# Decay, keys and token tiles moved ahead of the attention stage, recurrence spread along it: one step of a hybrid streaming encoder

## What is computed

```python
hp = ffn_step(hp, ...)                                  # macaron SwiGLU, 1024 -> 2816 -> 1024, layer norm
(q, k, v, qi, ki, wi), rec, gates = mixer_inputs(hp, w_in, lb)   # one projection, 5448 columns
oa   = attend_prompt(q, qi, wi, k, v, ki)               # index scores, top 256 keys per query, softmax over them
orec = recur_prompt(*rec)                               # HGRN2, 4 heads of 128x128 state
hp   = mixer_output(hp, oa, orec, gates, ...)           # rms norm of orec, gates, two projections, layer norm
hp   = ffn_step(hp, ...)

logf = log(lb + (1 - lb) * sigmoid(f));  kk = (1 - lb) * sigmoid(-f);  rq = silu(bq)
b = cumsum(logf)                                        # "decay", restarted in each block of 80 tokens
o = (q k^T * exp(b_t - b_s), causal) v + (q exp(b)) S
S = S * exp(b_end) + (k exp(b_end - b))^T v
```

## Time and profile before

| | us |
|---|---|
| median of three runs (2941.70 to 2948.98) | 2941.75 |
| the profiled execution's own time | 2947.6 |
| its span, first to last instruction | 2945.9 |
| first FFN | 0 to 837 |
| projection, index scores, search | 837 to 1448 |
| mixers | 1452 to 1862 |
| output projections, second FFN | 1862 to 2946 |

### The profile page before, as it was taken

The page is one execution under the profiler, slowest core; times in us unless marked ns, Lnnn a source line. Parts: engine busy times, 40 slices in busy tenths (PEclk is TensorE's granted clock), DMA queues, the critical chain, the costliest instruction groups (busy, mean ns, idle before and its releaser), DMA issues. The chain is left out here.

```text
span 2945.9 us, 41396 instructions
## 1 busy us (share of the span) xinstructions
PE 2730.8 (93%) x16384; PEld 2628.7 (89%) x16384; DVE 1341.0 (46%) x2842; ACT 668.3 (23%) x1135; POOL 485.8 (16%) x175
## 2 busy tenths in 40 slices
PE   8999999999977999999779986799999999999996
PEld 7999999999967799999768974699799999999995
DVE  2333333333254689992165437455543333333335
ACT  3111111111143522221255533200421111111102
POOL 1122111111010011222100002111111111222212
PEclk9999999999988999999859987799999999999998
DMA  4111111111021011232200000522011111111101
GB/s 146 44 43 43 48 55 54 43 43 30 1 71 44 15 44 44 96 95 89 97 1 31 1 1 8 183 75 80 29 44 43 43 43 43 43 43 44 55 16 60
DMA packets 143708, 149.13 MB, mean 51 GB/s; under 512 B 19648, under 2 KB 130336, under 8 KB 143472
## 3 DMA queue, kind: packets, MB, share of 16 engines
q1 hardware_dynamic: 140144, 134.45, 14.8%
q10 hardware_dynamic: 3456, 13.17, 1.1%
HBM read 123.82 MB, written 23.79 MB: 50 GB/s over the span
## 5 line engine op out<-in xcount | busy, mean ns | idle before, releaser
L475 DVE TENSOR_TENSOR ffn_prod<-ffn_gate,ffn_psu 128x384 f32<-128x384 f32 x132 | 69.5, 527 | 799.9 <-ACT ffn_gate L385 793.6
L67 PE MATMUL ffn_psd<-ffn_hid_hi,ffn_dn_hi 128*128 128x384 f32 (+1 forms) x1056 | 353.9, 335 | 12.7 <-DVE y L500 10.9
L67 PE MATMUL ixp_ps<-h_hi,ixp_hi 128*128 128x384 f32 (+1 forms) x1032 | 339.9, 329 | 20.2 <-ACT y L877 11.5
L67 PE MATMUL ffn_psg<-h_hi,ffn_up_hi 128*128 128x384 f32 (+1 forms) x1056 | 346.4, 328 | 8.4 <-DVE ffn_up_lo L400 6.6
L500 DVE TENSOR_TENSOR y<-y,ffn_psd 128x384 f32<-128x384 f32 (+1 forms) x480 | 250.9, 526 | 217.2 <-PE ffn_psd L69 217.2
L385 ACT ACTIVATE ffn_gate<-ffn_psg 128x384 f32<-128x384 f32 x132 | 61.9, 469 | 1259.3 <-PE ffn_psu L69 1259.2
L67 PE MATMUL ffn_psu<-h_hi,ffn_up_hi 128*128 128x384 f32 (+1 forms) x1056 | 344.0, 326 | 0.0
L68 PE MATMUL ffn_psg<-h_lo,ffn_up_hi 128*128 128x384 f32 (+1 forms) x1056 | 343.9, 326 | 0.0
L69 PE MATMUL ffn_psd<-ffn_hid_hi,ffn_dn_lo 128*128 128x384 f32 (+1 forms) x1056 | 343.8, 326 | 0.0
L68 PE MATMUL ffn_psd<-ffn_hid_lo,ffn_dn_hi 128*128 128x384 f32 (+1 forms) x1056 | 343.7, 325 | 0.0
L69 PE MATMUL ffn_psg<-h_hi,ffn_up_lo 128*128 128x384 f32 (+1 forms) x1056 | 343.1, 325 | 0.0
(11 more groups left out here) (299 smaller groups left out, 4995.5 us busy)
## 6 DMA issues: line engine op xcount, KB each, us to landing
ffn_dn_raw<-in_ffn_wd SPq DMA_DIRECT2D x22, 1024.0 KB, 4.9
ffn_up_raw<-in_ffn_wg SPq DMA_DIRECT2D x20, 1024.0 KB, 5.4
ffn_up_raw<-in_ffn_wu SPq DMA_DIRECT2D x20, 1024.0 KB, 7.8
ixp_raw<-in_w_in SPq DMA_DIRECT2D x39, 512.0 KB, 3.8
spill<-y ACTq DMA_DIRECT2D x24, 536.0 KB, 2.7
mo_sig<-spill SPq DMA_DIRECT2D x32, 192.0 KB, 3.8
y<-spill SPq DMA_DIRECT2D x2, 2144.0 KB, 8.3
y<-y_spill SPq DMA_DIRECT2D x1, 4288.0 KB, 15.0
```

Source lines behind the costliest of these rows:

```text
L67: pe.matmul(out, w_hi, x_hi, start=first, stop=False)
L475: dve.tensor_tensor(self.prod[:, k % 2, 0:w], self.gate[:, k % 2, 0:w], self.ps_up[k % banks][:, 0:w], ALU.mult).then_inc(self.prod_done, 1)
```

## The change

- **Projection order**: `PROJECTED` puts f and rq first, then ak, av, aq, ga and three gb, bi, the other gb, bg. The queries are spilled instead of bi; bi stays in SBUF (`c.y[:, 4:8]`), where the recurrence reads it. Still 24 tiles are spilled; the last nine go through a ring of two tiles in what was the search's scratch, and so wait for its end (`searched`).
- **Decay** becomes a class whose sigmoids and logs run on ACT after tile 10 of the projection (`decay`), whose sums run on DVE right after the search, and whose 32 exponentials and scalings are put among the chunks of the last eight tiles (`tail_order`, which PE, ACT and DVE follow). There too are the high and low keys (K) and the 18 key and value transposes (t, six groups, copied by DVE); SP stores the token rows at the end of that stage.
- **Mixers** begin with the first eight parts of the recurrence, then the three cache transposes (c), then attention. SP loads the queries back in three parts. The other 62 recurrence parts are spread evenly up to 94% of the attention's list, and the norm from there to 99%. In the norm ACT squares (q) and DVE multiplies with the gate (g); POOL has no part in it. The mask is no longer stored per head.

```diff
+SP = {"aq": 0, "ga": 4, "gb": 12, "bg": 20}
+PROJECTED = ([("iq", j) for j in range(4)] + [("ik", 0)] + [("f", j) for j in range(4)] + [("rq", j) for j in range(4)]
+             + [("ak", 0), ("av", 0)] + [("aq", j) for j in range(4)] + [("ga", j) for j in range(8)]
+             + [("gb", j) for j in range(3)] + [("bi", j) for j in range(4)] + [("gb", j) for j in range(3, 8)]
+             + [("bg", j) for j in range(4)])
+STEP_TILES = 8
+def tail_order():
+    chunks = [("P", n) for n in range(3 * STEP_TILES)]
+    out = []
+    for q in range(2 * Decay.NQ):
+        out.append(("e", q))
+        if q % 8 == 7:
+            out += chunks[0:3]
+            del chunks[0:3]
+    out += [("G", 0), ("K", 0)] + chunks[0:2]
+    del chunks[0:2]
+    for g in range(6):
+        out += [("t", g), chunks.pop(0)]
+    return out + chunks
+class Decay:
...
+    def grow_quarter(self, act, n):
+        h, t0 = self.quarters[n % self.NQ]
+        act.wait_ge(self.scanned, h + 1)
+        if n >= 2:
+            act.wait_ge(self.scaled, n - 1)
+        act.activation(self.grow[:, n % 2, :], self.fx[:, h, t0:t0 + T // 4], ACT.Exp,
+                       scale=1.0 if n < self.NQ else -1.0).then_inc(self.grown, 1)
...
     @block.scalar
-        for n in range(NI + EARLY // 3, NTL):
+        for n in range(NI + EARLY // 3, FIRST_STEP):
             for i in range(3):
                 drain(n, i)
+            if n == NI + 5:
+                dc.decay(act, s_mm, len(units))
+        for what, n in order:
+            if what == "P":
+                drain(FIRST_STEP + n // 3, n % 3)
+            elif what == "e":
+                dc.grow_quarter(act, n)
...
     @block.vector
+        dve.memset(bit_f[:], 0.0).then_inc(searched, 1)
+        for h in range(BH):
+            dc.sums(dve, h)
+        for what, n in order:
+            if what == "e":
+                dc.scale_quarter(dve, n)
...
-PACE = 1.22
+REC_SHARE, NORM_SHARE = 0.94, 0.99
 def pass_order(att_blocks, n_rec):
-    rec = [("g", h) for h in range(BH)] + [("e", q) for q in range(2 * 4 * BH)] + [("G", 0)]
-    rec += [("k", 0), ("v", 0), ("u", 0)]
+    rec = [("k", 0), ("v", 0), ("u", 0)]
     for m in range(n_rec):
         rec += [("k", m + 1), ("a", m), ("v", m + 1), ("o", m), ("u", m + 1)] if m + 1 < n_rec else [("a", m), ("o", m)]
-    rec += [("n", h) for h in range(BH)]
+    ahead = 8
+    norm = [x for h in range(BH) for x in [("q", h), ("n", h)] + [("r", 3 * h + i) for i in range(3)] + [("g", h)]]
+    out, done, normed = [("Q", 0)] + rec[0:ahead] + [("c", 0)], ahead, 0
     for i, part in enumerate(att):
         out.append(part)
+        while done < len(rec) and done - ahead < (len(rec) - ahead) * (i + 1) / (REC_SHARE * len(att)):
+            out.append(rec[done])
+            done += 1
+        while done == len(rec) and normed < len(norm) * min(1, (i / len(att) - REC_SHARE) / (NORM_SHARE - REC_SHARE)):
+            out.append(norm[normed])
+            normed += 1
+    return out
...
+                r.load_state(sp)
+                for part, spans in enumerate((((Q1, Q1 + QB),), ((Q1 + QB, LP),), ((LP, T), (0, Q1)))):
+                    for a, z in spans:
+                        sp.dma_start(c.aq[:, :, a:z], c.spill[SP["aq"]:SP["aq"] + 4, :, a:z].rearrange("n p t -> p n t")).then_inc(aq_in[part], 16)
```

More of the change, by code:

```diff
@@ L952, in index_and_project @@
     qs_set, dist_set, d = sem("qs"), sem("dist"), sem("d")
-    spilled = [sem(f"spilled{i}") for i in range(3)]
+    spilled, late_spilled = [sem(f"spilled{i}") for i in range(3)], [sem(f"late_spilled{i}") for i in range(2)]
+    searched = sem("searched")
     h_out = [sem(f"h_out{i}") for i in range(3)]
@@ L1000, in _ @@
         for n in range(4, NTL):
+            if n == NI + 6:
+                pool.wait_ge(s_mm, len(units))
+                dc.constants(pool)
             pr.split_lo(pool, n)
@@ L1187, in settled @@
             dve.wait_ge(d, done[0])
+        dc.bounds(dve)
         dve.wait_ge(dist_set, 1)
@@ L1342, in mixers @@
     units = [(b, h) for b in range(len(blocks)) for h in range(HEADS)]
-    NRT = NRB + 1
-    order = pass_order(len(blocks), NRT)
+    order = pass_order(len(blocks), Recurrence.NRT)
     piece_at, turn_at = {}, {}
@@ L1415, in mixers @@
[L1415 to L1423, removed]
@@ L1430, in by_head @@
[L1430 to L1431 removed]
+        Q1 = N_META + QB
         with nc.Block() as block:
@@ L1615, in make_stack @@
                     q0, m = blocks[b][0:2]
+                    for part in range(3 if b >= NB - 1 else 2 if b else 1):
+                        act.wait_ge(aq_in[part], 32 if part == 2 else 16)
                     if b >= 2:
@@ L1666, in _ @@
                 for what, n in order:
-                    if what == "Q" and n >= 1:
+                    if what == "k":
+                        r.keep_keys(act, n)
+                    elif what == "v":
+                        r.keep_values(act, n)
+                    elif what == "q":
+                        for i, (t0, w) in enumerate(CHUNKS):
+                            if n == 0:
+                                act.wait_ge(r.out_done, r.NRT)
+                            else:
+                                act.wait_ge(r_mm, 3 * n + i - 2)
+                            act.activation(sq[:, i, 0:w], rq[:, n, t0:t0 + w], ACT.Square).then_inc(sq_done, 1)
+                    elif what == "Q":
                         make_stack(n)
@@ L1810, in _ @@
                 for what, n in order:
-                    if what == "Q" and n >= 1:
+                    if what == "c":
+                        for m, (src, dst, rows) in enumerate(prep):
+                            dve.wait_ge(kv_mm, m + 1)
+                            dve.tensor_copy(dst, ps_t[m % 2][0:rows, 0:P]).then_inc(kv_done, 1)
+                        dve.tensor_copy(ks_t[:, PAST:NS], c.ak[:, LP:T]).then_inc(kv_done, 1)
+                    elif what == "a":
+                        r.mask(dve, n)
+                    elif what == "u":
+                        r.add(dve, n)
+                    elif what == "o":
+                        r.keep_out(dve, n)
+                    elif what == "Q":
                         stack_rests(n)
```

641 lines of the change are left out of this document (361 added, 280 removed).

## The result

The change takes 2960.13 us (median of 20 runs, 2942.66 to 2966.58) against 2948.55 for the kernel before (20 runs, 2941.20 to 2952.43): a ratio of 1.0041, interval 1.0030 to 1.0051. It is slower by 0.4%, just beyond what can be told from no change, where 2894 and faster were forecast. The profiled execution took 2959.26, its span was 2957.6.

What follows compares the result with a forecast made beforehand. PE bounds the projection's tail, DVE the mixers' start, where PE idles. Mixers ending at 1814 instead of 1862.5 save 48 us: 2947.6 becomes 2899, less 5.9 for the median, 2894; range 2876 to 2909 (0.62).

Steps and rivals of the forecast that it cites:

- does the clock rise early?: Start of the mixers: PE's clock expected up within some 10 us of the first recurrence parts, 1.00 from about 1485.
- one allowance of 7 us for all falls of the clock: Mixers' blocks: some 7 us added for clock falls, moving the recurrence's end from 1751 to 1758.
- The lengths given for the blocks at full clock: Attention blocks in the mixers: lengths without recurrence plus 5.6 us each while it runs, 273.2 us summed to the recurrence's end.
- Tile 10's stall: Projection: PE stalls 0 to 4 us, taken as 3, while drains wait behind the decay work on ACT.
- The tail's stall: Projection's last tiles: PE waits for a drain behind decay sums and exponentials, 0 to 6 us, taken as 2.
- The norm: Mixers' end, on DVE: reciprocals 28.6, scaling 7.1, gates 5, plus waits, 56 us; mixers end at 1814 instead of 1862.5.
- The recurrence's end: In the mixers: last recurrence output at 1758, allowance for clock falls included, against 1792.9 before.
- the forecast's last step: Whole kernel: from 2899 for a profiled execution to 2894, as the earlier one stood 5.9 us above the runs' median.
- The clock stays at 0.50: Rival, mixers' blocks: half speed for three blocks, 2946, no change (0.06); longer, 2970, slower (0.08).
- Coupling: Rival, mixers' units: one part order on three engines makes waits, 15 to 30 us given back, 2909 to 2924; chance 0.24.
- Stalls in the projection: Rival: both projection stalls in full with clock falls behind, 14 us instead of 7, 2901; no separate chance given.
- The change doesn't do what it says: Rival, mixers: a lagging recurrence would keep the norm from beginning at 94%; nothing showed that, no size or chance given.

Runs made afterwards that it cites:

- exp. 10: Combined run of four edits, plus the sample keys' high part and rests moved behind the fourth and fifth query stack: 2896.06 us, 0.9812 of the kernel before.
- exp. 1: Changed kernel with PE's value products of the unit before moved between second and third batch of turned tiles in nine-tile units: 2917.96 us, ratio 0.9897.
- exp. 3: Changed kernel with 18 unneeded identity transposes added in the gap of nine-tile units: 2933.63 us, 0.9947 of the kernel before.
- exp. 2: Changed kernel with the previous unit's value products made once more in the gap of nine-tile units: 2933.94 us, 0.9954 of the kernel before.
- experiment 4: Kernel before, with value products moved ahead of the third batch of turned tiles in nine-tile units: 2929.44 us, ratio 0.9940.
- experiment 6: Changed kernel with the recurrence spread over 70% of the attention's list instead of 94%, the norm over the rest: 2928.91 us, 0.9938 of the kernel before.
- experiment 8: Changed kernel with value products in the gap, tail drains first, recurrence over 70%, decay's sigmoids and logs singly behind drains of tiles 13 to 16: 2891.71 us, 0.9818.
- experiment 5: Changed kernel with the first tile's three drains ahead of the first eight decay exponentials in the last eight projection tiles: 2955.2 us, ratio 1.0026.
- experiment 9: Changed kernel with value products in the gap, tail drains first and decay pieces behind single drains, recurrence still over 94%: 2903.76 us, 0.9843.
- 11: Combined run of four edits, with the recurrence over 60% and the norm over 60 to 90% of the list: 2871.10 us, 0.9733 of the kernel before.

## Why the prediction was wrong

**The step that failed is "does the clock rise early?", and what was built on it: one allowance of 7 us for all falls of the clock.** From the first exponential to the mixers' end the change ran 210 us of 388.5 at 0.50, and its nine blocks took 59 us more than was forecast for them: 24 in the first three, 5 in the next three, 30 in the last three. The lengths given for the blocks at full clock were nearly right where a run shows them, but for the block with 1040 keys:

| block | forecast | change (clock) | at or near 1.00 elsewhere |
|---|---|---|---|
| first three | 21.6, 23.6, 26 | 32.6, 28.2, 34.4 (0.63, 0.88, 0.80) | 21.9, 26.6, 28.2 (exp. 10, 8.9 parts each) |
| fourth, fifth | 30, 34.3 | 31.5, 33.7 (1.00) | |
| sixth | 39.9 | 43.9 (0.94) | 39.2 (exp. 1) |
| 1040 keys | 57.8 | 68.7 (0.62) | 40.6 (exp. 1), 56.4 with filling (exp. 3) |
| sample | 19 | 29.1 (0.50) | 17.5 (exp. 2) |
| first query block | 18 | 26.9 (0.50) | none (23.4 at 0.67, exp. 3) |

For the block with 1040 keys the 57.8 was no length at full clock. Before, its clock was 0.89 over 63.1 us, which costs some 7 us; the sum took that cost off in the two blocks ahead of it and not here. Without the wait the block takes 40.6, and the 56.4 holds the added transposes.

*First scores* 17.5 us after the mixers' start, forecast 18.5: right. *Tile 10's stall*, 3.4, forecast 3: right. *The tail's stall*, 6.1 against "0 to 6 us, taken as 2": just above the range. The search ended at 1351.4, not at the 1347.6 of the earlier trace rows, and the sums took 22.3 us for 20, so that the first late drain came at 1378.3 and not by 1375; the mixers began 6.2 us later than forecast. *The norm*, 56 us forecast: 28.6, 7.1 and 5.1 on DVE, and the mixers end at 1873.0, some 54 us behind the last output of the recurrence: right. *The recurrence's end*, 1758 forecast: 1819.2. These 61 us (the blocks' 59, the later start and the last units, less the allowance of 7) are nearly the whole miss: the mixers' end, forecast at 1814, came 59 later. The other 6 are the forecast's last step: it took 5.9 us off because the profiled execution stood so far above a median of three runs. Over 20 runs the median of the kernel before is 2948.55, and the profiled 2947.6 lies below it, so that nothing was to be taken off.

**Where the reading went wrong.** From the earlier trace rows I took one fall and one quick return, "with recurrence in the stream", for the rule. The kernel before has three more such falls (at 1695, 1723 and 1743), each back within 7 us, so more of its rows would have said the same. In the change recurrence parts were in the stream from 1711 to 1819, and the clock did not come back until 1827. And I had the wait before the third batch, as a length that stays. It had a second price, the clock behind it, and the trace of before showed that: two of those falls stand 1.3 and 1.6 us behind this very wait, the first of them behind

```profile
1721.70 0.28 PE L1521 MATMUL mx_t<-ident,mx_prob 128*16 128x128 f32 x1 [1.71 <-ACT mx_prob_t L1659]
```

Both prices together were 19 us in the kernel before (experiment 4) and 42 in the change (experiment 1), with 12.9 and 6.6 recurrence parts in the block. That the thinner recurrence is the reason is not shown: experiment 6, with 8.9 parts to a block and recurrence nearly to that block's end, had as bad a one. Why the clock came back within 7 us there and not for 116 here stays open.

**The rivals.** *The clock stays at 0.50* was nearest, in kind and in number (no change at 2946, slower to 2970), though it was given 0.14 in all and the wrong place: it put the loss in the first blocks, where 44 of 95 us were low and 24 us of the miss lie, while the longest stretch, and 30 us, came at the end. *Coupling* is not it: blocks at 1.00 take what was summed or less, and adding work made the kernel faster (experiment 2). It survives as a cause of single waits: the 3.48 us of experiment 8, and the 1.71 us of the long block, where ACT's copy stood behind an exponential of another unit. *Stalls in the projection* were there in full, worth 5 us when one was removed (experiment 5). *The change doesn't do what it says*: it does.

With the three waits cured, the change's own schedule takes 2903.76 (experiment 9), inside the forecast's range and 10 above its number. That nearness is in part luck: its first three blocks take 94 us where 71 were forecast, and its long block 40.6 for 57.8, because the wait counted there is gone. What keeps the first block low at 94% (but not at 70 or 60%) is not settled.

## What to carry to other kernels

Price a wait of PE twice: its own length, and the half speed that may follow it; here waits of 8 us in one block went with 116 us at half clock, and filling the gap ahead of the ninth tile, even with useless transposes, took 26 us off. Before spreading filler work evenly, look at which gaps it fills now: move ready work into the gap first (one reordered call on one engine gave 42 us), then spread. And don't read from one quick recovery that the next will be as quick.

## What the runs showed of the hardware that was not expected

- The same blocks hold either level: the sample block at 1.00 takes 17.5 us, and at 0.50 PE is busy all 29.1 us without the clock's coming back.
- A fall came behind waits of 0.48, 1.71 and 1.71 us, with PE at work for most of the 6 us between them; with these gaps filled (experiments 2 and 3) the clock of that block was 0.97.
- In the gap, f32 transposes kept the granted clock as products did (56.4 and 57.9 us, both at 0.97).
- With a start 6.5 us earlier the clock's pattern was another in blocks whose instructions were the same: 0.68 for 0.88 in the second (experiment 5, one trace).
- Behind a wait of 3.5 us in the second block the clock fell (experiments 6 and 8); behind 1.4 and 1.5 us in that place it did not (experiments 10 and 11).
